# Two-layer transformer block on one core: stick-breaking weights as sums with value steps, outputs copied per head, positions as a column

## The chip, the cores and the metric

The kernel runs on one core of one Trainium2 chip. The metric is the device time of one execution in microseconds (us), the smaller the better. Five engines work side by side on their own instruction streams: TensorE (PE, matmuls, with its weight loads listed apart as PEld), VectorE (DVE), ScalarE (ACT), GpSimd (POOL) and SyncE (SP, which here only issues transfers). They meet through semaphores. Sixteen DMA engines move data between HBM and the on-chip memory, and within the latter.

## What is computed

A sequence of 512 tokens, 1024 wide, passes a hybrid layer (a state-space branch and a stick-breaking attention branch, gated and merged) and a second layer (sparse attention, a gated linear recurrence, a feed-forward net). The change is about two places. The first is the attention of the first layer, with 16 heads of 64:

```
log_fail = jnp.where(mask, jax.nn.log_sigmoid(-logits), 0.0)
between = lax.cumsum(log_fail, axis=3, reverse=True) - log_fail
w = jnp.where(mask, jnp.exp(jax.nn.log_sigmoid(logits) + between), 0.0)
outs.append(jnp.einsum('bhqk,bkhd->bqhd', w.astype(v.dtype), v[:, :kend]))
```

So the weight of key k is sigmoid(logit k) times the product of (1 - sigmoid) over the later keys. The second place is the compression of keys and values in the second layer, where a learned position is added to every block of 32 tokens before a matmul:

```
blocks = blocks + pos[None, None, :, None, :]
flat = blocks.transpose(0, 1, 3, 2, 4).reshape(B, ncmp, G, CMP_LEN * dh)
return jax.nn.gelu(flat @ w1) @ w2
```

## The kernel before

All fp32 weights are streamed in blocks of 1 MB (two pieces of 512 KB, `wraw`). ACT rounds a piece to `whi` (L1152), DVE takes the rest into `wlo` (L1481), and PE does three matmuls for each product (high by high, high by low, low by high), all at L739, which is the helper `mm`. `plan` writes down one list of steps; each engine runs through the same list and does its own part of every step. `weave` spreads two or more lists evenly through each other. So every engine has its order fixed in the program, and the engines wait only on semaphores.

The step ("sb", u) is one unit of the stick-breaking attention: u = 4 h + qt is head h and the query tile qt of 128 rows, with 128 (qt + 1) keys. The 64 units are woven with the slices of eight blocks of products `gate_ssd`, one slice (6 matmuls of 512 columns) a unit. In step u:

- PE: the logits of unit u in bank 4 or 5; the transposes of unit u - 2 (L1087) in bank 6; the products of unit u - 3 with the values, in a quarter of bank 7, which wait for the copy of the unit ahead (`s_o`).
- ACT: two sigmoids of unit u (L1287, L1288), a part of the next head's rounded keys and queries (`stack`, L1271 to L1275), the copy of the turned weights of unit u - 2 (L1297).
- DVE: the rests for the next head (L1902, L1905), a scan of unit u (L1925) that makes the products of "fail" from the last key down, and the copy of the output of unit u - 3 (L1932, 64 x 128).
- POOL: the product of the scan's result with the sigmoid (L2047). PE's transposes wait for it (`s_wgt`).

The values `vt` are read out of PSUM by ACT (L1226), four tiles for each half of the 16 heads: those of half 0 end in the middle of the steps that normalize y, those of half 1 just before unit 0. Results of the `gate_ssd` blocks are read by ACT (L1170) and DVE (L1537, kind `y_ssd`), into `mg`. The arena is one piece of memory of 96 KB a partition, in which tensors lie over each other in turn: `mg` starts at 16 KB, `sb_sig`, `sb_fail` and `sb_w` lie at 48, 52 and 57 KB.

In the second layer the step ("positions",) stands between the slices of the block `kv`. There PE multiplies 32 columns of positions with the compression weights `w1`, one row of output each; ACT copies the row (L1389), and `compress` (0) adds it to the blocks' products by a matmul of one row (`posr`, `one`). Around it, the tiles of the normed input `mix` are turned (PE, L800) and split (ACT L1262, DVE L1674), tile by tile.

Of the kernel before, what the change touches and what calls it, by code (L numbers as in the profile page):

```python
# [23 lines left out]
ALU = mybir.AluOpType  # L24
ACT = mybir.ActivationFunctionType
# [55 lines left out]
def plan():  # L81
# [93 lines left out]
    steps += kv[:2] + [("positions",)] + rows_[7] + kv[2:4] + rows_[8] + kv[4:5] + rows_[9] + kv[5:6] + rows_[10] + kv[6:]  # L175
# [77 lines left out]
def plan_tiles():  # L253
# [27 lines left out]
    groups = {"turn": (4, 6, 7), "dt": (7,), "level": (2, 3), "hout": (2, 3), "turn_qk": (2, 3), "hq": (0, 1), "hf": (0, 1)}  # L281
# [113 lines left out]
BANK_LOGITS, BANK_WT, BANK_O = 4, 6, 7  # L395

# [21 lines left out]
def emit(nc, dram, spill, out):  # L418
    ctx = ExitStack()
    with ctx:  # L420
# [85 lines left out]
        junks = {"x": mem(0, [NT, D]), "y": mem(52, [NT, D])}  # L506
# [9 lines left out]
        sb_fail = mem(52, [2 * 516])  # L516
        sb_w = mem(57, [3, T])
        sb_wT = mem(63, [2, T])
        zeros = mem(67.5, [1])
# [13 lines left out]
        kc2 = mem(24, [2, 2, T])  # L533
# [14 lines left out]
        posr = mem(55, [2 * P])  # L548
# [58 lines left out]
        s_qk, s_sig, s_scan, s_wgt = sem("s_logits"), sem("s_sb_sigmoids"), sem("s_sb_products"), sem("s_sb_weights")  # L607
# [129 lines left out]
        def _(pe):  # L737
# [97 lines left out]
            def positions():  # L835

                pe.wait_ge(s_late, 80)
                for b in range(2):
                    for j in range(CL // 2):
                        last = mm(bank[5][0:1, P * b:P * b + P], pos[:, b, j:j + 1], w1[b][:, j, :], j == 0, j == CL // 2 - 1)  # L840
                last.then_inc(s_pos, 1)

            def compress(i):

                if i == 0:
                    pe.wait_ge(s_kc2, 64)
                    pe.wait_ge(s_posr, 1)
# [45 lines left out]
            def nsa(u):  # L893
# [17 lines left out]
                def summed(v, b):  # L911
                    qt, h = divmod(v, NH)
                    out_ = bank[BANK_O]
                    if h == 0 and b == 0:
                        if qt == 0:
                            pe.wait_ge(s_cpt, NT)
                            pe.wait_ge(s_zero, 2)
# [146 lines left out]
            def stick(u):  # L1064
# [17 lines left out]
                if 0 <= v < SH * NT:  # L1082
                    pe.wait_ge(s_wgt, v + 1)
# [6 lines left out]
                if 0 <= v < SH * NT:  # L1090
# [3 lines left out]
                    if v >= 1:  # L1094
                        pe.wait_ge(s_o, v)
# [1031 lines left out]
```

## Time and profile before

| | |
|---|---|
| median of 3 runs | 1477.96 us (1476.66 to 1478.06) |
| profiled execution | 1475.07 us, of which the span from the first to the last instruction is 1473.2 us |
| PE busy | 1396.8 us (95%), 6981 matmuls |
| DVE busy | 770.7 us (52%) |
| ACT busy | 583.7 us (40%) |
| POOL busy | 178.2 us (12%) |
| mean granted clock of PE | 0.987 of full speed |
| DMA | 119.68 MB, 81 GB/s over the span |

The time follows PE: it is busy for most of the span, and the chain of work that ended last is 82% PE. A change of its order or a wait taken off another engine counts as far as PE stops waiting for it. The busy time of a matmul is longer than the distance to the next one, since they overlap.

### The profile page before, as it was taken

The numbers are of one execution on the slowest core, as the hardware profiler recorded it, in microseconds if no ns is written. First come the engines' busy times: TensorE is split into PE (matmuls) and PEld (weight loads), VectorE is DVE, ScalarE is ACT, GpSimd is POOL, SyncE is SP. The second block draws the span as 40 slices with busy tenths as digits, with TensorE's granted clock in tenths as the row PEclk, the third lists the DMA queues.
The fourth block names the chain that finished last, engine by engine and source line by source line (L and its number), as shares of the span: only waits on it lengthen the run. The fifth ranks groups of instructions, "written<-read, shape, count | busy, mean of one in ns | idle before, by whom it ended". The sixth has DMA issues, their size and how long they took to land.

```text
span 1473.2 us, 17942 instructions
## 1 busy us (share of the span) xinstructions
PE 1396.8 (95%) x6981; PEld 1137.7 (77%) x6981; DVE 770.7 (52%) x1198; ACT 583.7 (40%) x1061; POOL 178.2 (12%) x147
## 2 busy tenths in 40 slices
PE   6899999999999999998999989899989999999999
PEld 4778778877777788876787767677867888888887
DVE  5775454447776564345444657547743433443443
ACT  4544333456666433235325444343333221322221
POOL 0108430003333200000000122121000000000000
PEclk9999999999999999999999999999999999999999
DMA  4222212221111244322331100000522323233222
GB/s 155 84 74 63 81 60 98 86 86 58 44 44 57 70 175 137 107 83 68 139 113 58 44 15 29 15 15 1 172 71 73 100 91 108 88 100 101 93 93 101
DMA packets 34403, 119.68 MB, mean 81 GB/s; under 512 B 3856, under 2 KB 5136, under 8 KB 34064
## 3 DMA queue, kind: packets, MB, share of 16 engines
q1 hardware_dynamic: 33744, 117.50, 24.0%
q10 hardware_dynamic: 576, 1.05, 0.3%
q8 instruction: 56, 0.92, 0.2%
q14 instruction: 27, 0.22, 0.0%
HBM read 113.29 MB, written 4.19 MB: 80 GB/s over the span
## 4 chain that ended last, share of the span: by engine, by line
PE 82%; DVE 10%; ACT 4%; issue 3%; DMA 0%; POOL 0%; DVEq 0%; SPq 0%; ACTq 0%
PE bank L739 79%; DVE wlo L1481 1%; PE bank L800 1%; DVE arena L1925 1%; PE bank L908 1%; PE bank L1087 1%; DVE arena L1500 1%; ACT arena L1258 1%; DVE arena L1649 1%; DVE arena L1932 0%; DVE arena L1773 0%; ACT a_hi L1262 0%; DVE arena L1804 0%; ACT L1239 0%; ACT L1170 0%
## 5 line engine op out<-in xcount | busy, mean ns | idle before, releaser
L739 PE MATMUL bank<-a_hi,whi 128*128 128x512 f32 x848 | 341.8, 403 | 0.7 <-DVE a_lo L1674 0.7
L739 PE MATMUL bank<-a_hi,wlo 128*128 128x512 f32 x848 | 332.4, 392 | 0.0
L739 PE MATMUL bank<-a_lo,whi 128*128 128x512 f32 x848 | 331.7, 391 | 0.0
L1481 DVE TENSOR_TENSOR wlo<-wraw,whi 128x1024 fp32r<-128x1024 f32 x194 | 248.6, 1293 | 54.4 <-ACT whi L1152 48.9
L1152 ACT ACTIVATE whi<-wraw 128x1024 fp32r<-128x1024 f32 x194 | 197.1, 1045 | 184.3 <-PE bank L739 176.8
L739 PE MATMUL bank<-arena 128*128 128x128 f32 (+7 forms) x1400 | 221.4, 304 | 26.7 <-DVE arena L1932 10.1
L739 PEld LDWEIGHTS bank<-arena 128*128 128x128 f32 (+2 forms) x1400 | 175.8, 190 | 58.0 <-issue 29.5
L739 PEld LDWEIGHTS bank<-a_hi,wlo 128*128 128x128 f32 x848 | 160.0, 189 | 34.5
L739 PEld LDWEIGHTS bank<-a_hi,whi 128*128 128x128 f32 x848 | 160.6, 189 | 33.1 <-issue 2.0
L739 PEld LDWEIGHTS bank<-a_lo,whi 128*128 128x128 f32 x848 | 160.6, 189 | 31.7 <-issue 1.0
L739 PE MATMUL bank<-whi,a_hi 128*128 128x512 f32 x320 | 127.3, 398 | 5.2 <-DVE a_lo L1985 3.0
L739 PE MATMUL bank<-whi,a_lo 128*128 128x512 f32 x320 | 124.9, 390 | 0.0
L739 PE MATMUL bank<-wlo,a_hi 128*128 128x512 f32 x320 | 124.9, 390 | 0.0
L2047 POOL TENSOR_TENSOR arena<-arena 128x128 f32<-128x128 f32 (+1 forms) x64 | 67.1, 1053 | 229.6 <-DVE arena L1925 229.6
L739 PE MATMUL bank<-whi,b_hi 128*128 128x512 f32 x240 | 94.8, 395 | 0.0
L739 PE MATMUL bank<-whi,b_lo 128*128 128x512 f32 x240 | 94.1, 392 | 0.0
L739 PE MATMUL bank<-wlo,b_hi 128*128 128x512 f32 x240 | 94.1, 392 | 0.0
L1925 DVE TENSOR_TENSOR_SCAN arena<-arena 128x128 f32<-128x128 f32 (+1 forms) x64 | 54.2, 847 | 50.5 <-ACT arena L1288 50.3
L739 PEld LDWEIGHTS bank<-whi,a_hi 128*128 128x128 f32 x320 | 60.4, 189 | 18.1 <-issue 6.2
L1201 ACT ACTIVATE b_hi<-arena 128x512 fp32r<-128x512 f32 x30 | 19.0, 632 | 135.6 <-DVE arena L1584 123.7
L2040 POOL TENSOR_TENSOR arena<-arena,stat 128x256 f32<-128x256 f32 (+3 forms) x32 | 40.1, 1253 | 254.4 <-DVE stat L1734 254.4
L1574 DVE TENSOR_TENSOR arena<-arena,bank 128x512 f32<-128x512 f32 x32 | 22.0, 687 | 92.4 <-PE bank L739 92.4
(236 smaller groups left out, 1769.0 us busy)
## 6 DMA issues: line engine op xcount, KB each, us to landing
wraw<-in_wblk SPq DMA_DIRECT2D x190, 512.0 KB, 3.7
arena<-in_x SPq DMA_DIRECT2D x4, 512.0 KB, 5.6
arena<-in_x SPq DMA_DIRECT2D x1, 2048.0 KB, 8.3
spill<-arena SPq DMA_DIRECT2D x4, 512.0 KB, 6.7
arena<-spill SPq DMA_DIRECT2D x1, 2048.0 KB, 9.8
out<-arena SPq DMA_DIRECT2D x8, 256.0 KB, 2.5
arena<-in_w1k SPq DMA_DIRECT2D x1, 1024.0 KB, 7.2
arena<-in_w1v SPq DMA_DIRECT2D x1, 1024.0 KB, 6.0
```

The source lines that it names most:

```text
L739: return nc.tensor.matmul(o, lhsT, rhs, start=start, stop=stop, **kw)
L800: last = nc.tensor.transpose(bank[BANK[g]][:, P * i:P * i + P], src[:, t, c0 + P * i:c0 + P * i + P], ident)
L908: last = nc.tensor.transpose(bank[BANK_WT][:, o:o + P], np_[v % 3][:, b_, P * kb:P * kb + P], ident)
L1087: last = nc.tensor.transpose(bank[BANK_WT][:, P * kb:P * kb + P], sb_w[:, v % 3, P * kb:P * kb + P], ident)
L1152: A(whi[n % 2][:, cols], wraw[i][:, 0:cols.stop - cols.start], ACT.Copy).then_inc(s_hi, 1)
L1201: A(b_hi[:, c, :], tt[:, p % 2, :], ACT.Copy).then_inc(s_tround, 1)
L1258: A(junk[:, t, :], src[:, t, :], ACT.Square, accum_out=nss[name][:, t:t + 1]).then_inc(s_ss, 1)
L1481: v.tensor_tensor(wlo[n % 2][:, cols], wraw[i][:, 0:cols.stop - cols.start], f32(whi[n % 2][:, cols]), ALU.subtract).then_inc(s_lo, 1)
L1574: v.tensor_tensor(x, x, ps[:, :], ALU.add).then_inc(s_end["V"], 1)
L1925: v.tensor_tensor_scan(w[:, ::-1], fail[:, ::-1], zeros.to_broadcast([P, kend]), 1.0, ALU.mult, ALU.add)\
L2040: g_.tensor_tensor(w, w, f2[:, 2 * (u % 2):2 * (u % 2) + 2].unsqueeze(2).to_broadcast(list(w.shape)), ALU.mult)\
L2047: g_.tensor_tensor(w, w, sb_sig[:, u % 2, 0:kend], ALU.mult).then_inc(s_wgt, 1)
```

## The change

In the attention, the weights are no longer formed. The sum over keys of weight times value is written by parts: the scan now runs state = fail x state + sigmoid, from 0, which gives for each key the sum of the weights of this and all later keys, and the values are replaced by their steps from one token to the next, v(k) - v(k - 1). The product by POOL goes, and PE's transposes wait for the scan (`s_scan`).

The steps need the value of the token before, which lies on the partition before. So ACT, when it has read the last tile of a half, issues two transfers from on-chip memory to on-chip memory into `v_before[half]`: 127 partitions x 4 x 512, shifted by a partition, and the 3 rows that cross from one tile to the next. POOL zeroes the first row ahead, and subtracts behind (128 x 2048 a half, `s_dv`). `v_before[0]` lies at 52 KB, over `sb_fail` and `sb_w`; `v_before[1]` lies at 16 KB, under `mg`. So ACT's first sigmoid waits for `s_dv` 1, and DVE's first read of a `y_ssd` tile waits for `s_dv` 2.

The outputs of a head stay in one bank, 7 for even and 3 for odd heads, and DVE copies them once a head (64 x 512). The `gate_ssd` tiles use banks 0 to 2 only. The first `z_sb` block waits for the last head's copy.

The positions become a 65th column of the compression's input (`kc2`), so the step ("positions",) and the matmuls of one row go; ACT copies two columns out of PSUM and adds them as the bias of the Gelu. Other sizes, loops and blocks stay.

```diff
-    steps += kv[:2] + [("positions",)] + rows_[7] + kv[2:4] + rows_[8] + kv[4:5] + rows_[9] + kv[5:6] + rows_[10] + kv[6:]
+    steps += kv[:2] + rows_[7] + kv[2:4] + rows_[8] + kv[4:5] + rows_[9] + kv[5:6] + rows_[10] + kv[6:]
...
-    groups = {"turn": (4, 6, 7), "dt": (7,), "level": (2, 3), "hout": (2, 3), "turn_qk": (2, 3), "hq": (0, 1), "hf": (0, 1)}
+    groups = {"turn": (4, 6, 7), "dt": (7,), "level": (2, 3), "hout": (2, 3), "turn_qk": (2, 3), "hq": (0, 1), "hf": (0, 1),
+              "gate": (0, 1, 2), "y_ssd": (0, 1, 2)}
...
+BANKS_STICK = (7, 3)
...
-        junks = {"x": mem(0, [NT, D]), "y": mem(52, [NT, D])}
+        junks = {"x": mem(0, [NT, D]), "y": mem(60, [2, 512])}
...
+        v_before = [mem(52, [NT, 512]), mem(16, [NT, 512])]
...
+                if TILES[g][0] == "z_sb":
+                    pe.wait_ge(s_o, SH)
...
                     for b in range(2):
-                        o = bank[4][:, 64 * b:64 * b + 64].rearrange("p (a b) -> p a b", b=32)[:, :, 0:NCMP]
                         for j in range(CL // 2):
-                            mm(o, w1[b][:, j, :], kc2[:, b, :, 2 * j:2 * j + CS * (NCMP - 1) + 1:CS], j == 0, False)
-                        last = mm(o, posr[0:1, P * b:P * b + P], one[0:1, 0:2 * NCMP].rearrange("p (a b) -> p a b", b=NCMP),
-                                  False, True)
+                            last = mm(bank[4][:, P * b:P * b + 2 * 32 + 1], w1[b][:, j, :],
+                                      kc2[:, b, 2 * j:2 * j + CS * 2 * 32 + 1:CS], j == 0, j == CL // 2 - 1)
...
-                    pe.wait_ge(s_wgt, v + 1)
+                    pe.wait_ge(s_scan, v + 1)
...
-                    if v >= 1:
-                        pe.wait_ge(s_o, v)
+                    if qt == 0:
+                        pe.wait_ge(s_dv, 1 + h // 8)
+                        if h >= 2:
+                            pe.wait_ge(s_o, h - 1)
                     for kb in range(qt + 1):
-                        last = mm(bank[BANK_O][:, P * (v % 4):P * (v % 4) + P], vt[:, kb, pair],
+                        last = mm(bank[BANKS_STICK[h % 2]][:, P * qt:P * qt + P], vt[:, kb, pair],
                                   sb_wT[:, v % 2, P * kb:P * kb + P], kb == 0, kb == qt)
...
                     A(vt[:, t, 512 * half:512 * half + 512], ps[:, :], ACT.Copy).then_inc(s_end["S"], 1)
+                    if t == NT - 1:
+                        cols = slice(512 * half, 512 * half + 512)
+                        act.wait_ge(*ended(g))
+                        act.wait_ge(s_vz, half + 1)
+                        act.dma_start(v_before[half][1:P, :, :], vt[0:P - 1, :, cols]).then_inc(s_vs[half], 16)
+                        act.dma_start(v_before[half][0:1, 1:NT, :], vt[P - 1:P, 0:NT - 1, cols]).then_inc(s_vs[half], 16)
...
-                        act.wait_ge(s_wgt, u - 1)
+                        act.wait_ge(s_scan, u - 1)
+                    if u == 0:
+                        act.wait_ge(s_dv, 1)
...
+                    A(pos_bias, bank[4][:, 64:64 + P + 1:P], ACT.Copy).then_inc(s_posr, 1)
+                    act.wait_ge(s_posr, 1)
...
                     if kind == "y_ssd":
+                        if i == 0:
+                            dve.wait_ge(s_dv, 2)
                         v.tensor_tensor(mg[:, i, :], ps[:, :], sg, ALU.mult).then_inc(s_end["V"], 1)
...
-                    v.tensor_tensor_scan(w[:, ::-1], fail[:, ::-1], zeros.to_broadcast([P, kend]), 1.0, ALU.mult, ALU.add)\
+                    v.tensor_tensor_scan(w[:, ::-1], fail[:, ::-1], sig[:, ::-1], 0.0, ALU.mult, ALU.add)\
                         .then_inc(s_scan, 1)
...
-                if 0 <= o:
-                    h, qt = divmod(o, NT)
+                if 0 <= o and o % NT == NT - 1:
+                    h = o // NT
...
-                    v.tensor_copy(qf[rows_, h // 2, P * qt:P * qt + P], bank[BANK_O][rows_, P * (o % 4):P * (o % 4) + P]).then_inc(s_o, 1)
+                    v.tensor_copy(qf[rows_, h // 2, :], bank[BANKS_STICK[h % 2]][rows_, :]).then_inc(s_o, 1)
...
-                if s[0] == "sb" and s[1] < SH * NT:
-                    u = s[1]
-                    kend = P * (u % NT + 1)
-                    pool.wait_ge(s_scan, u + 1)
-                    w = sb_w[:, u % 3, 0:kend]
-                    g_.tensor_tensor(w, w, sb_sig[:, u % 2, 0:kend], ALU.mult).then_inc(s_wgt, 1)
+                if s[0] == "stack":
+                    turned = max(SPLITS.index(x) for x in SPLITS if x[:2] == ("turn", "y")) + 1
+                    for half in range(2):
+                        if half == 1:
+                            pool.wait_ge(s_split, turned)
+                        else:
+                            pool.wait_ge(s_y, NT)
+                        g_.memset(v_before[half][0:1, 0, :], 0.0).then_inc(s_vz, 1)
+                    for half in range(2):
+                        steps_ = vt[:, :, 512 * half:512 * half + 512]
+                        pool.wait_ge(s_vs[half], 32)
+                        g_.tensor_tensor(steps_, steps_, v_before[half], ALU.subtract).then_inc(s_dv, 1)
```

What the change does to the order on ACT, at the end of the values and the start of unit 0. Before (L1226 reads a value tile, L1287 and L1288 are the sigmoids of unit 0, the table load in between is ACT's change of function):

```order
L1226 ACTIVATE arena<-bank 128x512 [waits s_tile_summed] x2
L1287 ACT_TABLE_LOAD [waits s_zero]
L1287 ACTIVATE arena<-bank 128x128 [waits s_logits]
L1288 ACTIVATE arena<-bank 128x128
L1271 ACTIVATE rounded_arena<-arena 64x512
```

The same place in the changed kernel (L1228 and L1229 are the two transfers, `s_value_steps` is `s_dv`):

```order
L1223 ACTIVATE arena<-bank 128x512 [waits s_tile_summed] x2
L1228 DMA arena<-arena 127x4x512 [waits s_before_first_zero,s_tile_read_s]
L1229 DMA arena<-arena 1x3x512
L1289 ACT_TABLE_LOAD [waits s_value_steps]
L1289 ACTIVATE arena<-bank 128x128 [waits s_logits]
L1290 ACTIVATE arena<-bank 128x128
L1274 ACTIVATE rounded_arena<-arena 64x512
```

Two transfers have come between, and all that ACT does from unit 0 on stands behind a wait for POOL's first subtraction. The same pair of transfers stands behind the last value tile of half 0, further up.

On DVE, around the first `y_ssd` tile, which comes in unit 7. Before (L1925 is the scan, listed here as SCALAR_TENSOR_TENSOR; L1932 copy of an output, L1905 a rest for the next head, L1537 the `y_ssd` tile):

```order
L1925 SCALAR_TENSOR_TENSOR arena<-arena 128x384 [waits s_sb_turned,s_sb_sigmoids]
L1932 COPY arena<-bank 64x128 [waits s_sb_summed]
L1905 TENSOR_TENSOR rounded_arena<-arena,rounded_arena 64x512 [waits s_stacks_rounded]
L1925 SCALAR_TENSOR_TENSOR arena<-arena 128x512 [waits s_sb_turned,s_sb_sigmoids]
L1932 COPY arena<-bank 64x128 [waits s_sb_summed]
L1537 TENSOR_TENSOR arena<-bank,arena 128x512 [waits s_tile_read_s,s_tile_summed]
```

In the changed kernel (L1924 scan, L1931 copy of a head, L1909 the rest, L1541 the `y_ssd` tile):

```order
L1924 SCALAR_TENSOR_TENSOR arena<-arena 128x384 [waits s_sb_turned,s_sb_sigmoids]
L1931 COPY arena<-bank 64x512 [waits s_sb_summed]
L1909 TENSOR_TENSOR rounded_arena<-arena,rounded_arena 64x512 [waits s_stacks_rounded]
L1924 SCALAR_TENSOR_TENSOR arena<-arena 128x512 [waits s_sb_turned,s_sb_sigmoids]
L1541 TENSOR_TENSOR arena<-bank,arena 128x512 [waits s_value_steps,s_tile_read_s,s_tile_summed]
L1924 SCALAR_TENSOR_TENSOR arena<-arena 128x128 [waits s_sb_turned,s_sb_sigmoids]
```

The copies between scans have gone down to one a head, and the `y_ssd` tile, ahead of the scan of unit 8, now waits for POOL's second subtraction.

## Rows read from the trace of the kernel before

**Rows 1.** Waits of PE between 324 and 510 us: total, times, longest.

```profile
PE bank L739 <- DVE arena L1932: 10.1, 17, 0.8
PE bank L739 <- DVE rounded_arena L1905: 1.7, 8, 0.6
PE bank L1087 <- POOL arena L2047: 0.2, 1, 0.2
```

**Rows 2.** Timeline: start us, duration us, engine, line, operation [idle before, releaser].

```profile
353.51 1.82 DVE L1481 TENSOR_TENSOR wlo<-wraw,whi 128x1024 fp32r<-128x1024 f32 x1
356.19 0.41 PE L739 MATMUL bank<-rounded_arena 128*128 128x128 f32 x2 [0.15 <-DVE rounded_arena L1905]
356.44 0.23 PE L739 MATMUL bank<-cstb 128*128 128x128 bf16 x1
356.51 0.50 PE L1087 MATMUL bank<-cst,arena 128*128 128x128 f32 x3
357.33 0.28 DVE L1932 COPY arena<-bank 64x128 f32<-64x128 f32 x1
357.76 0.68 PE L739 MATMUL bank<-arena 128*128 128x128 f32 x4 [0.76 <-DVE arena L1932]
...
368.85 0.68 PE L739 MATMUL bank<-arena 128*128 128x128 f32 x4 [0.44 <-DVE arena L1932]
```

**Rows 3.** Stretches: length, busy PE, PEld, DVE, ACT, POOL, granted clock, DMA share, GB/s.

```profile
357.00:380.00 23.00, 21.55 (x133) 17.77 (x132) 16.34 (x24) 15.45 (x35) 8.30 (x8) 1.00 0.15 47
1055.00:1108.00 53.00, 45.31 (x200) 36.87 (x198) 24.77 (x36) 16.95 (x27) 0.00 (x0) 0.92 0.25 80
```

**Rows 4.** Groups by line: the scans; busy us, mean ns | idle before.

```profile
L1925 DVE TENSOR_TENSOR_SCAN arena<-arena 128x128 f32<-128x128 f32 (+1 forms) x64 | 54.2, 847 | 50.5 <-ACT arena L1288 50.3
```

**Rows 5.** Timeline: last value tile of half 0, units 0 and 8.

```profile
300.06 0.60 ACT L1226 ACTIVATE arena<-bank 128x512 f32<-128x512 f32 x1 [2.04 <-PE bank L739]
...
325.61 0.28 ACT L1287 ACTIVATE arena<-bank 128x128 f32<-128x128 f32 x1
...
345.84 0.69 DVE L1537 TENSOR_TENSOR arena<-bank,arena 128x512 f32<-128x512 f32 x1
346.44 0.67 DVE L1925 TENSOR_TENSOR_SCAN arena<-arena 128x128 f32<-128x128 f32 x1
...
351.09 0.28 PE L1087 MATMUL bank<-cst,arena 128*128 128x128 f32 x1
```

**Rows 6.** DMA view of 742 to 750 us, where `kcf` goes to `kc2`.

```profile
DMA packets 576, 1.05 MB, mean 131 GB/s; under 512 B 64, under 2 KB 320, under 8 KB 576
...
q10 hardware_dynamic: 576, 1.05, 56.8%
```

**Rows 7.** DMA queue of the page: packets, MB, share of 16 engines.

```profile
q1 hardware_dynamic: 33744, 117.50, 24.0%
```

**Rows 8.** DMA view of 352 to 358 us, 40 slices: GB/s of the weights' load.

```profile
GB/s 0 0 0 0 0 0 0 0 0 0 0 0 0 0 0 0 0 0 0 0 0 0 0 0 0 0 0 0 137 109 82 191 218 246 410 328 382 410 410 246
```

**Rows 9.** Views of single lines: ACT's issues of `kc2`, POOL's 128 x 1024 products; ns min/median/max.

```profile
L1216 ACTq DMA_DIRECT2D arena<-arena x4: 617/704/1352, 742.8 to 744.9; - x4
...
L2022 POOL TENSOR_TENSOR arena<-arena,stat x4: 1899/1904/2352, 109.9 to 185.7; 128x1024 f32<-128x1024 f32 x4
```

**Rows 10.** Timeline around the step of the positions.

```profile
699.79 7.15 PE L739 MATMUL bank<-arena,cst 128*1 128x128 f32 x64
704.32 1.22 DVE L1481 TENSOR_TENSOR wlo<-wraw,whi 128x1024 fp32r<-128x1024 f32 x1
...
711.00 1.29 DVE L1674 TENSOR_TENSOR a_lo<-bank,a_hi 128x512 fp32r<-128x512 f32 x2 [5.47 <-ACT a_hi L1262]
711.84 0.47 PE L739 MATMUL bank<-whi,a_hi 128*128 128x512 f32 x1 [1.07 <-DVE a_lo L1674]
715.26 1.09 PE L800 MATMUL bank<-cst,arena 128*128 128x128 f32 x8 [0.41 <-DVE arena L1649]
```

**Rows 11.** Timeline at the start of the compression.

```profile
771.10 0.43 PE L739 MATMUL bank<-cst,arena 1*128 1x62 f32 x2
```

More of the change, by code:

```diff
@@ L532, in emit @@
         kcf = mem(48, [2, T])
-        kc2 = mem(24, [2, 2, T])
+        kc2 = mem(23.75, [2, 2 * T + CL])
         w1 = [mem(56, [CL // 2, P]), mem(72, [CL // 2, P])]
@@ L547, in emit @@
         nsq = mem(54.25, [P])
-        posr = mem(55, [2 * P])
+        pos_bias = mem(55, [2])
         np_ = [mem(kb, [2, T]) for kb in (24, 28, 60)]
@@ L606, in emit @@
         s_attn, s_yd, s_y, s_st = sem("s_ssd_attn"), sem("s_y_diag"), sem("s_y_read"), sem("s_state")
-        s_qk, s_sig, s_scan, s_wgt = sem("s_logits"), sem("s_sb_sigmoids"), sem("s_sb_products"), sem("s_sb_weights")
+        s_qk, s_sig, s_scan = sem("s_logits"), sem("s_sb_sigmoids"), sem("s_sb_sums")
+        s_vz, s_dv = sem("s_before_first_zero"), sem("s_value_steps")
+        s_vs = [sem(f"s_values_shifted{i}") for i in range(2)]
         s_tr, s_wT, s_pv, s_o = sem("s_sb_turned"), sem("s_sb_wT"), sem("s_sb_summed"), sem("s_sb_out")
@@ L833, in qkturn @@
                 last.then_inc(s_tile, 1)
[L835 to L841, printed above, removed]
             def compress(i):
@@ L1111, in _ @@
                     qkturn(*s[1:])
-                if s[0] == "positions":
-                    positions()
                 if s[0] == "compress":
@@ L1215, in tile @@
                             for later in range(2):
-                                act.dma_start(kc2[HD * later:HD * later + HD, :, g_, 0:T - later],
+                                act.dma_start(kc2[HD * later:HD * later + HD, :, T * g_:T * g_ + T - later],
                                               kcf[HD * g_:HD * g_ + HD, :, later:T]).then_inc(s_kc2, 16)
@@ L1254, in norm @@
                         cols = slice(512 * g, 512 * g + 512)
-                        last = A(junk[:, t, cols], src[:, t, cols], ACT.Square, accum_out=nss[name][:, 2 * t + g:2 * t + g + 1])
+                        last = A(junk[:, g, :], src[:, t, cols], ACT.Square, accum_out=nss[name][:, 2 * t + g:2 * t + g + 1])
                     last.then_inc(s_ss, 1)
@@ L1387, in _ @@
                     round_small("gates")
-                    act.wait_ge(s_pos, 1)
-                    A(posr[0:1, :], bank[5][0:1, 0:2 * P], ACT.Copy).then_inc(s_posr, 1)
                 if s[0] == "qkturn":
@@ L1914, in stick @@
                     if u == 0:
-                        for i in range(2):
-                            v.memset(sb_fail[:, 516 * i + 512:516 * i + 513], 1.0)
-                        v.memset(zeros, 0.0).then_inc(s_zero, 1)
-                        dve.wait_ge(s_zero, 1)
                         v.memset(zerob[:, :], 0.0).then_inc(s_zero, 1)
@@ L1948, in _ @@
                 if s[0] == "pos":
+                    dve.wait_ge(s_late, 80)
+                    v.tensor_copy(kc2[:, :, 2 * T:2 * T + CL:2], pos).then_inc(s_pos, 1)
                     v.tensor_scalar(V("q_norm"), V("q_norm"), SCALE, None, ALU.mult)
```

22 lines of the change are left out of this document (9 added, 13 removed).

## The prediction

> **What bounds the kernel now.** I read the page first: PE is busy for nearly the whole span, so only what PE waits for, or what is put in its way, can change the time. Then the waits of PE in the attention stage, 324 to 510 us [rows 1]: 10.1 us for DVE's copies of the outputs, 1.7 us for the next head's rest, and only 0.2 us for POOL. The product by POOL is thus not on the path, though the change is named for it; the copies are, since the products of a unit may not begin before the last unit's copy, and DVE has a scan ahead of that copy. The timeline shows one such place [rows 2]: the transposes start at 356.51, DVE's copy ends at 357.61, the products start at 357.76, after 0.76 us of idle. The pattern comes back every 22.9 us (two heads), with a second, smaller wait (0.44 us at 368.85) and 0.15 us before the logits at 356.19.
>
> **What the change takes out of the attention.** Without a wait a matmul starts some 0.16 us before the listed end of the one ahead (356.44 + 0.23 against 356.51 [rows 2]), so a wait costs its idle time and 0.16. From unit 8 on (346 us) there are 7 waits of 0.76, 6 of 0.44 and 7 of 0.15: 7 x 0.92 + 6 x 0.60 + 7 x 0.31 = 12.2 us. The first two kinds go, since the products now wait for a copy two heads back. The third goes as well: the rest of the next head was late behind an L1481 of 1.82 us [rows 2], and without POOL's work beside it I expect that near the 1.22 of [rows 10]. DVE is busy for 16.3 us of such a stretch of 23 and ACT for 15.5 [rows 3], so neither becomes the bound; the scan with two real operands I take as long as before, a mean of 847 ns [rows 4] (bounds: no change, and twice that, a rival below). The first two heads give 0.9 + 0.6 more, if nothing else holds them. At the end of the stage the last head's copy (as the 0.69 us of L1537 [rows 5]) must end before `z_sb` begins, while POOL's product leaves that path: I set this to nothing, between 0.5 of gain and 0.7 of loss.
>
> **What the change adds: the shifted values.** This is the term that decides. The last tile of half 0 is read at 300.06 to 300.66 [rows 5]. Then 127 x 4 x 512 floats, 1.04 MB, go from on-chip memory to on-chip memory. ACT's first sigmoid, now at 325.61, waits for that and for POOL; DVE's first `y_ssd` tile, now at 345.84 [rows 5], waits for the second half. The question is how long such a transfer takes. The nearest one is that of `kc2`: 576 packets, 64 of them under 512 B, for 4 transfers of 128 rows [rows 6]. So each sends 128 rows and 16 small packets, one for each of the 16 engines that share it, 8 rows each. All transfers of this kernel have 128 or 64 partitions, which 16 divides. Of 127 rows no equal share is possible but one engine with all of them, or 127 with one. No row shows what happens then, so I bound it. Shared by 16 engines as `kc2` was, the 1.04 MB take the 8 us of that window at most. On one engine they take what the engines together were busy for: 0.568 x 16 x 8 = 73 us by `kc2`'s rate [rows 6]; 0.240 x 16 x 1473.2 / 117.5 x 1.04 = 50 us by that of the weights [rows 7]; 41 us at the best slices of a load, 410 GB/s by 16 engines, 25.6 each [rows 8]. I take one engine, and 50 us: the lone transfer has no fifteen neighbours to share the memory's ports with, as `kc2` had, but meets the weights' own packets on its engine.
>
> The Trainium skill has a rule for this, in "DMA: Bandwidth & Descriptors", section "Why a DMA increments its semaphore by 16 and not by 1": a transfer from ACT's or SP's queue is spread over the largest number of engines up to 16 that divides the slowest dimension of both sides, and 127 partitions get a single engine. What this case's trace has, 16 small packets each for transfers of 128 rows, agrees, and no run here yet shows 127. By the bandwidth per engine in that page's table (some 27 GiB/s) the 1.04 MB would take about 36 us, an estimate, and the sum below would come to about 1488; the rates in the rows are lower.
>
> The two halves use the same queue and engine, so the second waits for the first: they land at 300.7 + 50 = 350.7 and 400.7. POOL's subtraction of 128 x 2048 costs two of the 1.90 us in [rows 9], 3.8. The first sigmoid comes near 355 (29 us late), the first `y_ssd` tile at 404.5 where it stood at 345.84: 58.7 us late, and this second wait holds the first within it. What is queued behind: DVE's scan of unit 8 and all later scans; PE's transposes of unit 8 wait for it. PE has some room: the scan ended at 347.1, the transposes began at 351.09 [rows 5], so 4.0 us are taken up. PE comes out 54.7 us late. Having stood still it starts at a lower clock: the stretch from 1055 to 1108, with waits in it, was granted 0.92 on the mean [rows 3], 4 us lost in 53; for the one restart that counts I take 2 us (0 to 4). ACT's issues cost 0.7 us each at the median, 1.35 at most [rows 9]; in this case the wait covers them.
>
> The shared queue of weights feels the second stream on one engine only, 8 of its packets a piece; its loads have slack in a stage that stands still.
>
> **What the change takes out of the second layer.** The step of the positions holds PE for 7.1 us from 699.79 on [rows 10]. What follows doesn't simply move up, since DVE's split of the next tile queues behind its L1481, which ends at 705.54, where it now begins at 711.00 [rows 10]. So the split begins 5.5 us earlier, and the rest of that chain (matmuls 711.84, turn 715.26) hangs on it: 5.5 us gained, of 7.1 at most, 4 at least if DVE has more ahead. The two pairs of one-row matmuls cost 0.35 us each (771.10 to 771.45 [rows 11]); ACT's copy of two columns and its wait give back some 0.3, and the 65th column next to nothing: 0.4 gained. The rest of the second layer is PE without waits, or unchanged.
>
> **Sum.** +54.7 + 2 - 12.2 - 5.5 - 0.4 = +38.6. Against the profiled execution of 1475.07 that is 1513.7; the median of the runs lies 2.9 above that execution, so 1516.5, say 1516.
>
> **The rivals.**
>
> *The transfers are shared by many engines* (the other side of the bound). Then the first half lands by 309 and is subtracted by 313, ahead of 325.61; the second, issued at 324.3, is subtracted by 337, ahead of 345.84. What stays: -12.2 - 1.5 for the first heads - 5.5 - 0.4, and 0.7 of ACT's two issues at the start: -18.9, 1459. It decides as soon as a transfer takes under some 17 us (324.3 + 0.7 + 17 + 3.8 = 345.8). For it: nothing in the trace says that 127 is refused an uneven share. Against: all transfers shown go in equal parts. Chance 0.15.
>
> *Slow packets.* One engine, but at `kc2`'s rate of 73 us: `y_ssd` at 300.7 + 146 + 3.8 = 450.5, so 46 us more, 1562. For it: `kc2` is the only transfer of this kind shown, with the same rows of 2 KB. Against: its sixteen engines ran against each other. Chance 0.12.
>
> *ACT is held by its issue.* 508 rows for one engine may keep ACT at the issue until most are taken; the fourth issue of `kc2` took twice as long as the others [rows 9]. Then ACT stands for nearly 50 us at 300.7 and again at 324: 100 less about 8 of room, less the 20 of the gains: +72, 1550. Against: the rows of one transfer have never held it for more than 1.35 us. Chance 0.13.
>
> *Fast packets*, 41 us: 2 x 9 less, 1498. This is within the likeliest case, as its lower end.
>
> *The scan with two operands is slower*, so that DVE bounds the stage: twice as long, the scans add 54.2 / 8 = 6.8 us for two heads [rows 4] to the 16.3 in 23 and take back the 12 us: 1528. Chance 0.03, within the range.
>
> **How the numbers follow.** One engine, ACT free, 41 to 60 us a transfer: 0.55, 1516, by itself 1497 to 1536. With the rivals above on the slow side (0.28) the range goes to 1568. Below 1495 lies only the shared transfer (0.15) and a little (0.02) between, such as an uneven split over few engines. A measurement of this kernel tells about 0.2% (3 us) from no change. Faster 0.16, same 0.01, slower 0.83.
>
> **What would show it.** Right: landing times of some 50 us for the two transfers; POOL's subtractions near 351 and 401; the first sigmoid behind the first, the `y_ssd` tile behind the second, PE idle for two long stretches; from there on 21.1 us for two heads instead of 22.9, with no wait for the copies; 5.5 us less between the slices of `kv`. Wrong: landings of 5 to 8 us, and no wait for `s_dv` on ACT or DVE. Then the time is near 1459. If ACT has issues of tens of us, it is the third rival.

## The result, and the profile after

The changed kernel takes 1530.45 us (median of 4 runs, 1529.01 to 1531.42) against 1477.31 us (1476.54 to 1478.06) for the kernel before on the same chip: 53.1 us more, ratio 1.036 with a 95% interval of 1.0343 to 1.0376. The profiled execution took 1531.42 us, of which the span is 1529.6.

The page of the profile after: busy time of PE, and the chain that ended last, by line.

```profile
PE 1392.8 (91%) x6909; PEld 1138.3 (74%) x6913; DVE 757.2 (49%) x1148; ACT 582.1 (38%) x1061; POOL 121.7 (8%) x87
...
PE bank L743 76%; ACTq L1229 4%; PE bank L1084 1%; PE bank L806 1%; PE bank L905 1%; DVE arena L1502 1%; DVE wlo L1483 1%; ACT arena L1261 1%; ACT whi L1149 0%; DMA arena<-in_x 0%; DVE arena L1653 0%; DVE arena L1777 0%; DVE arena L1808 0%; ACT a_hi L1265 0%; ACT L1167 0%
```

PE does 4 us less work than before and is idle for the rest. New in the chain is one line with 4%: L1229, an *issue* of a DMA, by ACT. That is the transfer of three rows. The timeline of ACT after, at the place of [rows 5] (L1223 reads a value tile, L1228 issues the 127 rows, L1229 the 3 rows, L1289 is the first sigmoid):

```profile
301.30 0.60 ACT L1223 ACTIVATE arena<-bank 128x512 f32<-128x512 f32 x1 [2.04 <-PE bank L743]
301.93 1.32 ACTq L1228 DMA_DIRECT2D arena<-arena  x1
303.28 34.09 ACTq L1229 DMA_DIRECT2D arena<-arena  x1
337.42 0.60 ACT L1265 ACTIVATE b_hi<-bank 128x512 fp32r<-128x512 f32 x1 [35.52 <-issue]
...
359.91 0.60 ACT L1223 ACTIVATE arena<-bank 128x512 f32<-128x512 f32 x1 [2.12 <-PE bank L743]
360.54 0.74 ACTq L1228 DMA_DIRECT2D arena<-arena  x1
361.32 34.71 ACTq L1229 DMA_DIRECT2D arena<-arena  x1
396.11 1.28 ACT L1289 ACT_TABLE_LOAD   x1 [35.60 <-issue]
397.40 0.28 ACT L1289 ACTIVATE arena<-bank 128x128 f32<-128x128 f32 x1
```

The big transfer is issued in 1.32 us. The next issue on the same queue holds ACT for 34.1 us, and in the second half for 34.7. Read against [rows 5], the delay can be followed: the last value tile of half 0 is read 1.2 us later than before, the last tile of half 1, which stood at 323.69, comes 36.2 later, and the first sigmoid (325.61 before) 71.8 later. PE waits twice, at the turn of the next y tile (L806) and for the first sigmoids (L1290), which must free a bank of logits. Waits of PE after, 296 to 520 us:

```profile
PE bank L743 <- ACT arena L1290: 33.5, 1, 33.5
PE bank L806 <- DVE arena L1650: 33.4, 1, 33.4
PE bank L743 <- ACT arena L1223: 0.9, 1, 0.9
PE bank L1084 <- DVE arena L1924: 0.4, 1, 0.4
```

The 17 waits for copies and the 8 for a head's rest [rows 1] are gone. The stretches after, in the columns of [rows 3]: the two holds, what followed the second, and two heads in full swing:

```profile
303.00:338.00 35.00, 7.37 (x35) 5.83 (x33) 0.00 (x0) 0.58 (x2) 0.00 (x0) 0.64 0.07 25
361.00:396.00 35.00, 3.42 (x18) 2.53 (x17) 0.00 (x0) 0.00 (x0) 0.00 (x0) 0.59 0.08 30
396.00:419.00 23.00, 20.67 (x117) 17.07 (x118) 17.72 (x18) 18.27 (x39) 5.10 (x1) 0.88 0.18 56
430.00:453.00 23.00, 23.00 (x145) 19.31 (x144) 13.70 (x18) 16.12 (x36) 0.00 (x0) 1.00 0.21 65
```

The DMA view of 303 to 338 us shows what moves while ACT is held (the first row is GB/s in 40 slices, q10 is ACT's queue):

```profile
GB/s 12 37 14 26 26 26 26 26 26 23 26 23 26 26 23 26 26 23 26 23 26 26 23 26 23 26 26 23 26 26 23 26 26 23 26 23 26 26 23 26
...
q10 hardware_dynamic: 414, 0.85, 6.4%
```

A flat 25 GB/s, and a share of 6.4% of sixteen engines, which is 1/16 and no more: one engine works and fifteen stand still. POOL, which waits for both transfers of a half, shows when they have landed:

```profile
349.50 4.61 POOL L2054 TENSOR_TENSOR arena<-arena 128x2048 f32<-128x2048 f32 x1
405.08 5.10 POOL L2054 TENSOR_TENSOR arena<-arena 128x2048 f32<-128x2048 f32 x1 [50.98 <-DMA arena<-arena]
```

The first of them shows only that the landing was over by 349.5: POOL's memset of 0.52 us, which had waited for DVE, stands right ahead of it. The second waited for the transfer itself, until 405.1. So the landings are at most 47.5 us and 44.5 us behind the starts of their issues.

### The profile page after: what moved, and what is told of

Its sections match the earlier page's. It is cut to its first block, busy times and chain, and to the rows that moved or that the text cites. A ratio compares the mean times of both kernels' runs of the same rounds, so it can differ in the third digit from the quotient of the medians.

```text
span 1529.6 us, 17658 instructions
## 1 busy us (share of the span) xinstructions
PE 1392.8 (91%) x6909; PEld 1138.3 (74%) x6913; DVE 757.2 (49%) x1148; ACT 582.1 (38%) x1061; POOL 121.7 (8%) x87
## 4 chain that ended last, share of the span: by engine, by line
PE 79%; DVE 9%; ACTq 5%; ACT 4%; issue 2%; DMA 0%; SPq 0%; DVEq 0%
PE bank L743 76%; ACTq L1229 4%; PE bank L1084 1%; PE bank L806 1%; PE bank L905 1%; DVE arena L1502 1%; DVE wlo L1483 1%; ACT arena L1261 1%; ACT whi L1149 0%; DMA arena<-in_x 0%; DVE arena L1653 0%; DVE arena L1777 0%; DVE arena L1808 0%; ACT a_hi L1265 0%; ACT L1167 0%
## 5 line engine op out<-in xcount | busy, mean ns | idle before, releaser
L743 PEld LDWEIGHTS bank<-a_hi,whi 128*128 128x128 f32 x848 | 161.0, 190 | 34.1 <-issue 2.0
L1924 DVE TENSOR_TENSOR_SCAN arena<-arena 128x128 f32<-128x128 f32 (+1 forms) x64 | 56.9, 890 | 93.7 <-ACT arena L1290 93.4
L806 PE MATMUL bank<-cst,arena 128*128 128x128 f32 x144 | 26.5, 336 | 60.8 <-DVE arena L1650 33.8
L806 PEld LDWEIGHTS bank<-cst,arena 128*128 128x128 f32 x144 | 21.3, 174 | 67.2 <-DVE arena L1650 34.6
L743 PEld LDWEIGHTS bank<-whi,a_lo 128*128 128x128 f32 x320 | 61.4, 192 | 13.2
```

Of the source, the lines that this page charges most:

```text
L743: return nc.tensor.matmul(o, lhsT, rhs, start=start, stop=stop, **kw)
L806: last = nc.tensor.transpose(bank[BANK[g]][:, P * i:P * i + P], src[:, t, c0 + P * i:c0 + P * i + P], ident)
L1924: v.tensor_tensor_scan(w[:, ::-1], fail[:, ::-1], sig[:, ::-1], 0.0, ALU.mult, ALU.add)\
```

## The experiments

**The parts alone, and the transfer without its size of 127.** Four kernels on one chip; before took 1476.54 us (1475.3 to 1478.05, 15 runs). One row less in the big transfer:

```diff
-act.dma_start(v_before[half][1:P, :, :], vt[0:P - 1, :, cols]).then_inc(s_vs[half], 16)
+act.dma_start(v_before[half][1:127, :, :], vt[0:126, :, cols]).then_inc(s_vs[half], 16)
+act.dma_start(v_before[half][127:128, :, :], vt[126:127, :, cols]).then_inc(s_vs[half], 16)
```

> The changed kernel with one row less in each big transfer: 126 rows in one transfer and the 127th row in one of its own, so three issues a half and not two; all else as it is. Theory A (the number of rows decides: 127 has no divisor up to 16 but 1, 126 is divided by 14): the 126 rows go over 14 engines, each sends 36 rows of 2 KB where one sent 508, so a half lands within 4 to 8 us, no issue holds ACT for more than 1.4 us, and neither the first sigmoid nor the first y_ssd tile waits; with the gains of the rest that is 1459 us (1456 to 1465). Theory B (the shift by a partition, or the way within on-chip memory, makes the transfer slow, whatever its rows): the 126 rows take 45 us as the 127 did, ACT is held behind them, and the time stays near 1530 us. Theory C (the extra transfers and POOL's subtraction matter by themselves): between, 1480 to 1510 us.

Measured: 1465.49 us (1464.99 to 1467.59), ratio 0.9928 (0.9916 to 0.9941). A single row decides between 3.6% slower and 0.7% faster. That is theory A in kind, 0.5 us above its range. In the DMA view of 300 to 310 us the same megabyte goes by within 6 us, and its packets take 34% of sixteen engines' time. In the timeline the second half's three issues take 0.93, 0.64 and 1.61 us (I had set 1.4 as the most):

```profile
q10 hardware_dynamic: 532, 1.05, 34.1%
```

```profile
326.67 0.93 ACTq L1228 DMA_DIRECT2D arena<-arena  x1
327.63 0.64 ACTq L1229 DMA_DIRECT2D arena<-arena  x1
328.30 1.61 ACTq L1230 DMA_DIRECT2D arena<-arena  x1
330.31 1.28 ACT L1290 ACT_TABLE_LOAD   x1 [3.67 <-issue]
```

The order of the two transfers turned round, the 3 rows first:

> The changed kernel with the two transfers of a half in the other order: the 3 rows first, the 127 rows behind them. In the changed kernel the issue of the 127 rows took 1.3 us and the next issue, of the 3 rows, 34 us. Theory A (an issue is held while the queue still has the rows of the one ahead, so the hold belongs to whatever is issued next): ACT is free after half 0's big issue at about 304 us, is held at half 1's small issue from about 324 to 337 us, and issues the big one then; it lands 45 us behind the first half's landing at 347, so near 392, POOL has subtracted by 397.5, and the first y_ssd tile stands there where it stood at 416.1: 18.6 us less than the changed kernel, 1512 us (1508 to 1518), which is the case that the prediction took as the likeliest. Theory B (the hold is the cost of the small transfer itself): ACT is held for 34 us at the first small issue as well, and the time stays near 1530 us. Theory C (ACT stands behind the big transfer whatever comes next, and the hold only shows at the next instruction): the big issue is followed by 34 us of ACT idle, and the time stays near 1530 us.

Measured: 1515.54 us (1514.83 to 1517.14), ratio 1.0267 (1.0253 to 1.0281). That is theory A: ACT goes on at once behind the big transfer, and is held at its next issue, whatever that is. Here that is the small transfer of half 1, 22 us later (timeline of ACT; the first of its lines is half 0's big issue):

```profile
302.89 0.77 ACTq L1229 DMA_DIRECT2D arena<-arena  x1
303.71 0.60 ACT L1265 ACTIVATE b_hi<-bank 128x512 fp32r<-128x512 f32 x1 [2.21 <-PE bank L806]
...
325.45 19.77 ACTq L1228 DMA_DIRECT2D arena<-arena  x1
345.25 0.72 ACTq L1229 DMA_DIRECT2D arena<-arena  x1
358.93 1.28 ACT L1289 ACT_TABLE_LOAD   x1 [33.51 <-POOL arena L2054]
```

The hold ended at 345.2 and not at 337 as I expected: the stream shared its engine with four loads of weights here, where in the changed kernel no load ran during the first hold. POOL's subtractions began at 354.4 and 399.9, and the first `y_ssd` tile waited 25.5 us for the second and stood at 404.5, 11.6 us earlier than in the changed kernel. The 19.8 us of the hold cost nothing of their own. The landing that ACT's sigmoid waits for came later still, and the second transfer was in the queue by 346.0, while some 100 rows of the first were still to go, so it did not start later for the hold.

The positions alone, on the kernel before:

> The kernel before with one part of the change alone: the positions as a 65th column, no step of the positions, Gelu with a bias; attention as before. Theory A (the DVE split of the next tile hangs on the L1481 ahead of it, and moves up by 5.5 us; 0.4 from the one-row matmuls): 5.9 us less than before, ratio 0.9960. Theory B (what the two traces show between the turns around this place, 21.4 us before and 16.8 after): 4.6 us less, with 0.4 for the compression 5.0, ratio 0.9966. Theory C (the weights' stream or DVE's order takes it back later): 0 to 2 us less. Theory D (all 7.1 us of the step are gained): 7.5 us less, ratio 0.9949.

Measured: 1472.89 us (1472.57 to 1474.73), ratio 0.9977 (0.9968 to 0.9986): 3.65 us less, by the interval 2.1 to 4.7. The timeline of PE behind the turn (L800) that follows the removed step:

```profile
703.94 1.04 PE L800 MATMUL bank<-cst,arena 128*128 128x128 f32 x8
707.80 0.47 PE L739 MATMUL bank<-whi,a_hi 128*128 128x512 f32 x1 [2.83 <-DVE a_lo L1663]
...
709.05 0.63 PE L739 MATMUL bank<-whi,a_lo 128*128 128x512 f32 x1
```

The wait for the split grew from 1.07 [rows 10] to 2.83, as the working said. What it did not have is the third line: 1.2 us behind that wait the matmuls begin to take 0.63 us, and start 0.42 apart, where they took 0.39 and started 0.23 apart: the lower of PE's two clock levels, 1.2 GHz (granted 0.92 on the mean of 697 to 718 us; 1.00 in the like stretch before, 696 to 717). From the turn ahead of the place to the first matmul behind the turn that follows it are 16.8 us (697.52 to 714.33) where there were 21.4 (696.00 to 717.41), a gain of 4.6. In the compression the one-row matmuls are gone, but PE then waits 1.02 us for the Gelu where it waited 0.17, because ACT copies the two columns first: 0.1 of gain instead of 0.4. That is theory B for the place. Place and compression together make 4.7, which lies at the edge of the interval. In the median 1 us is missing, and where it went is not shown.

The copies alone:

> The kernel before with one part of the change alone: two banks for the outputs, one copy a head of 64 x 512, gate_ssd tiles on banks 0 to 2; scan from 1, POOL's product with the sigmoid and the positions as before, values as they are. Theory A (the waits for the copies were the whole cost, 10.1 us with 0.16 us of restart for each, and the 0.15 us waits before the logits stay or go): 10 to 14 us less than before, ratio 0.9905 to 0.9932, and the waits of PE for the copies vanish from the stage. Theory B (POOL's product, which stands between scan and transposes, becomes the next bound once the copies are gone): waits of PE for POOL of several us take their place, and 2 to 7 us are gained. If A holds, writing the weights as sums with steps of values buys nothing by itself.

Measured: 1465.52 us (1464.84 to 1466.73), ratio 0.9925 (0.9912 to 0.9939): 11.0 us less. That is theory A. Waits of PE, 324 to 510 us (L1936 is the copy of the last head, L1909 the rest, L2051 POOL's product):

```profile
PE bank L741 <- DVE rounded_arena L1909: 1.7, 8, 0.6
PE bank L1091 <- POOL arena L2051: 1.2, 1, 1.2
PE bank L741 <- ACT arena L1230: 0.9, 1, 0.9
PE bank L741 <- DVE arena L1936: 0.9, 1, 0.9
```

10.1 us of waits for copies became 0.9. The 1.7 for the rests stayed: they do not hang on the copies. In the changed kernel, without POOL's product, they are gone.

**What is left of the split kernels.** The parts add to 1461.9; the kernel with 126 and 1 rows has them all and takes 3.6 more. Four kernels on one chip (before 1477.35, 1476.43 to 1481.17).

> The changed kernel with 14 rows less in each big transfer: 113 rows in one and 14 in a second; all else as it is. 113 is a prime number as 127 is, 126 is not. Theory A (only the divisors of the number of rows decide how many engines a transfer gets): the 113 rows go over one engine again, though 14 rows were taken off where one row was enough with 126; they take 113/127 of the 45 us, 5 us less a half, and the hold at the next issue is 5 us shorter as well: 1530.5 less 10, 1520 us (1515 to 1526). Theory B (127 is a special case, a full tile less one row, or it is a matter of the last row alone): 113 rows are spread as 126 were, and the time is 1465 us.

Measured: 1521.53 us (1520.97 to 1522.02), ratio 1.03 (1.0285 to 1.0316). That is theory A, to 1.5 us: 113 rows go over one engine like 127, and the holds are 29.49 and 30.29 us.

> The changed kernel with each big transfer in 112 and 15 rows, over 16 and 15 engines by the divisors, where the run with 126 and 1 had 14 and 1. Theory A (with many engines the transfer itself is off the path; what is left over the sum of the parts, 1461.9, is the three issues ahead of unit 0 on ACT, 3.6 us of PE's wait for the first scan): the same time as the 126 and 1, 1465.5 us (1463.5 to 1467). Theory B (the single row on one engine and the 14 engines were a part of the rest): 1461 to 1463 us.

Measured: 1467.75 us (1466.19 to 1469.69), ratio 0.9937 (0.9922 to 0.9952). It is no better than 126 and 1, 0.75 us above the range of theory A, and by ratio not told apart from 126 and 1: the lone row was no part of the rest.

> The kernel before with both parts that gained by themselves, the copies a head and the positions as a column, and without the third: scan from 1, POOL's product, values as they are, no shifted values. Theory A (the parts add: 11.0 and 3.65 us less, from 1476.5): 1461.9 us, ratio 0.990, and so 3.6 us better than the changed kernel with its transfers split well, which has every part. Theory B (the sums with steps save something that the two parts alone don't, such as POOL's 0.2 and 1.2 us of wait): equal to the split kernels, 1465 us or more.

Measured: 1462.33 us (1460.87 to 1463.59), ratio 0.9899 (0.9885 to 0.9914). That is theory A: the two parts add.

The issues moved to POOL (the same transfers, in POOL's program, with half 0 subtracted before half 1 is issued):

> The changed kernel with the shifted values in three transfers a half (112, 15 and the 3 rows), all issued by POOL, which stands idle there, instead of ACT, and with POOL's subtraction of half 0 ahead of the transfers of half 1. Theory A (ACT's issues of 3.3 us ahead of the table load and the first sigmoid are what the split kernels still lose): the first sigmoid comes 3.3 us earlier than at 331.6, near 328, PE's wait of 3.6 us for the first scan goes, and the time is 1461 to 1462.5 us. Theory B (POOL's issues take longer than ACT's, 5 us or more a transfer): the second half is then subtracted after 345.8, the first y_ssd tile waits for it, and the time is 1465 to 1480 us.

Measured: 1465.2 us (1464.34 to 1465.76), ratio 0.9917 (0.9901 to 0.9934). By its time it is neither theory A nor, by its cause, theory B. The first sigmoid moved up to 326.36, earlier than A had it, POOL's issues took 0.5 to 1 us, and the time stayed. The timelines of POOL and DVE say why (L2053 subtraction, L1903 a head's rest, L1672 the split of a y tile, read from PSUM):

```profile
310.49 4.63 POOL L2053 TENSOR_TENSOR arena<-arena 128x2048 f32<-128x2048 f32 x1 [6.68 <-DMA arena<-arena]
...
332.56 4.52 POOL L2053 TENSOR_TENSOR arena<-arena 128x2048 f32<-128x2048 f32 x1 [5.22 <-DMA arena<-arena]
```

```profile
310.99 0.69 DVE L1672 TENSOR_TENSOR b_lo<-bank,b_hi 128x512 fp32r<-128x512 f32 x1 [1.92 <-ACT b_hi L1259]
...
332.63 5.00 DVE L1903 TENSOR_TENSOR rounded_arena<-arena,rounded_arena 64x512 fp32r<-64x512 f32 x1
```

The rest of a head, 0.69 us elsewhere, took 5.00, and ended 0.55 behind POOL's subtraction; PE waited 4.2 us for it. The split L1672, with one operand in PSUM, ran beside the other subtraction in its normal 0.69. The Trainium skill states this as a rule ("SBUF — State Buffer", section "SBUF: two separate sides"): DVE and GpSimd share a pair of ports that the first to start holds for its whole instruction, and a DVE operation wants it when both of its inputs are in SBUF. The rows agree on both counts.

**The subtraction in pieces.** The same two kernels with POOL's instruction of 128 x 2048 made of sixteen; before took 1476.31 us (1475.08 to 1477.67).

```diff
-g_.tensor_tensor(steps_, steps_, v_before[half], ALU.subtract).then_inc(s_dv, 1)
+for piece in range(16):
+    a, b = piece // 4, slice(P * (piece % 4), P * (piece % 4) + P)
+    last = g_.tensor_tensor(steps_[:, a, b], steps_[:, a, b], v_before[half][:, a, b], ALU.subtract)
+last.then_inc(s_dv, 1)
```

> The kernel with 126 and 1 rows (1465.5 us), with one change: each of POOL's two subtractions of 128 x 2048 is made of 16 instructions of 128 x 128. In the 126 and 1 kernel the second subtraction ran from 333.66 to 338.19, and DVE's two scans that began at 334.36 show 5.22 us where they should take 1.4; PE waited 3.6 us for them. Theory A (a single long POOL instruction keeps DVE out of the on-chip memory for its whole length, and short ones let it in between): no DVE instruction there is longer than 2 us, the wait of 3.6 us shrinks to below 1, and the time is 1462 to 1463.5 us. Theory B (the 3.6 us come from ACT's three issues ahead of the first sigmoid, 3.3 us): the time stays at 1465 to 1466 us. Theory C (16 instructions with their fixed costs, 16 x 0.46 = 7.4 us, are as long as one, and DVE is slowed for as long): 1465 us or more, with several DVE instructions a little longer.

Measured: 1465.63 us (1462.92 to 1466.74), ratio 0.9925 (0.9911 to 0.9939). The scans beside POOL are down from 5.22 for two to 0.97 and 1.04, and PE's wait from 3.6 to 1.6. But the median is that of theory B, and the five runs lie 3.8 us apart. The trace is of an execution of 1463.47 us, 2.2 below the median, and the one it is compared with was the slowest of its five, at 1467.59. With ACT's issues in place this run settles nothing by its time.

> The kernel in which POOL issues the transfers (112, 15 and 3 rows; 1465.2 us), with each subtraction of POOL in 16 instructions of 128 x 128. There the first sigmoid came at 326.4 as it should, and yet PE waited 4.2 us, for a DVE instruction (the rest for the next head, 64 x 512) that took 5.00 us, from 332.63 on, where others of it take 0.69, beside POOL's subtraction of 332.56 to 337.08. Theory A (DVE is kept out for the length of one POOL instruction): this wait goes, and the time is 1461 us (1459.5 to 1462.5), the best with all parts of the change in it. Theory B (it is the amount of POOL's work that slows DVE): 1464 to 1466 us. If A holds here and not with ACT's issues, both causes are in the rest.

Measured: 1458.54 us (1458.28 to 1459.64), ratio 0.9882 (0.9866 to 0.9897). That is theory A in kind, 1 us below its range. The same DVE instruction beside POOL's pieces:

```profile
332.02 0.84 DVE L1903 TENSOR_TENSOR rounded_arena<-arena,rounded_arena 64x512 fp32r<-64x512 f32 x1
```

PE's waits of 296 to 510 us come to 2.0 us in all. The 6.7 us between the two medians are more than the wait of 4.2: the stretch from 324 to 346 us was granted 0.84 of the full clock with the whole subtraction and 1.00 with the pieces, which is up to 3.5 us more (0.16 x 22, an estimate). So a stop of DVE for some 4 us cost PE its wait and, behind the wait, part of its clock. By the time, both causes are in the rest: pieces alone (with ACT's issues) and POOL's issues alone each left it at 1465, both together took it away. This is the fastest of the kernels run. Against copies and positions alone, 1462.33, which had its own runs of before, the intervals of the two ratios just overlap; if the 3.8 us between the medians are real, they are what the sums with steps buy by themselves, and the rows have 2.9 for them: the waits for the rests (1.7) and for POOL's product (1.2), which copies and positions alone still have, are gone.

> The kernel with POOL's issues and subtractions in pieces, but with the 127 rows in one transfer again, as in the changed kernel; so only the engine that issues it differs, and the size of the subtraction's pieces. Theory A (the transfer of 127 rows goes over one DMA engine whoever issues it): 45 us each, ACT is never held, the first y_ssd tile waits until both have landed and are subtracted, near 395 to 400 (or later, if POOL issues the second only behind the subtraction of the first, at about 354: then 354 + 45 + 7 = 406), and the time is 1515 to 1525 us. Theory B (POOL's queue divides a transfer in another way than ACT's, over all engines): no wait of its own, and the same time as with 112 and 15 rows, near 1461 us.

Measured: 1541.7 us (1540.09 to 1542.51), ratio 1.0441 (1.0426 to 1.0456). That is theory A in kind, 17 us above its range. Timeline of POOL:

```profile
301.25 4.78 POOL L2048 DMA_DIRECT2D arena<-arena  x1 [68.07 <-ACT arena L1223]
306.04 0.55 POOL L2049 DMA_DIRECT2D arena<-arena  x1
359.89 6.62 POOL L2054 TENSOR_TENSOR arena<-arena 128x128 f32<-128x128 f32 x16 [53.31 <-DMA arena<-arena]
...
367.71 4.61 POOL L2048 DMA_DIRECT2D arena<-arena  x1 [0.74 <-POOL arena L2044]
372.32 0.53 POOL L2049 DMA_DIRECT2D arena<-arena  x1
422.86 6.62 POOL L2054 TENSOR_TENSOR arena<-arena 128x128 f32<-128x128 f32 x16 [50.01 <-DMA arena<-arena]
```

Counted from the start of the issue, as for ACT's queue, POOL's transfers take 58.6 and 55.2 us where ACT's took 47.5 and 44.5. The issue of the 127 rows is 4.6 to 4.8 us long, where that of 112 rows costs 0.8 to 1. The DMA view of 305 to 340 us has the rest of the difference (q0 is POOL's queue, q1 that of the weights):

```profile
DMA packets 4569, 2.70 MB, mean 77 GB/s; under 512 B 3917, under 2 KB 3917, under 8 KB 4569
q0 software_dynamic: 3993, 0.60, 20.9%
```

Where 112 and 15 rows made 320 packets a half, 127 rows make some 4100, nearly all of them under 512 B. From 306 to 315 us they take 66% of sixteen engines' time and move 0.12 MB. The load of weights issued meanwhile lands after 12.1 us, where the median is 3.7. The rows themselves go only behind them, over one engine: from 330 to 345 us the queue takes 5.9% of sixteen. What the small packets are for is not shown. And the second transfer starts only at 367.7, so the two waits add: the `y_ssd` tile stands at 429.6, where I had 406.

## Why the prediction held, and which of its steps did not

**One engine for 127 rows** was the step that decided, and it is shown: 6.4% of sixteen engines in the changed kernel, 34% with one row less. 113 rows behave like 127, 126 and 112 like 128. The packets of ACT's queue say it to the engine. A half has 511 rows, and by [rows 6] each transfer adds one small packet for each engine that shares it. The queue sent 515 packets with 127 + 3 rows, 529 with 113 + 14 + 3, 532 with 126 + 1 + 3, and 545 with 112 + 15 + 3. That is 4, 18, 21 and 34 small ones: 1 + 3, 1 + 14 + 3, 14 + 4 + 3 and 16 + 15 + 3 engines. The page cited there, section "Why a DMA increments its semaphore by 16 and not by 1" of "DMA: Bandwidth & Descriptors" in the Trainium skill, gave this rule; the trace agrees for every size run (the lone row goes by its next dimension, of 4). **The rate**, taken as 50 us, was at most 47.5 and 44.5. The best slices of a load [rows 8], 25.6 GB/s an engine, were the right row: a lone transfer runs at 25. The 41 us of that row were its pure time, without the start and the small transfer behind. With loads of weights on the same engine, as in the run with the small transfer first, the first landing came 51.5 us behind its issue, near the 50 of the forecast.

**ACT free** is the step that failed. I took the issue of the 127 rows as done in a microsecond, which it is, and gave 0.13 to ACT being held by it. What happened is that rival, with the hold moved one issue further and shorter: the *next* issue waits until most of the rows are gone. When ACT came free, 406 and 407 of 508 packets had gone in the changed kernel, and 350 and 354 of 452 with 113 rows: each time 98 to 102 were left. So a hold takes 34 us and not 50. The rival's sum, redone with it: two waits of PE, 33.4 + 33.5, less the 14.65 that copies and positions give by themselves, is 52.3; measured 53.1. With ACT free at that place, as in the run with the small transfer first, the time was 1515.5, the 1516 of my forecast, and it came by the forecast's path: landings one behind the other, by 354.4 and 399.9 (350.7 and 400.7 forecast), and the `y_ssd` tile at 404.5. What is luck there are terms that cancel: PE waited 31.4 + 21.5 = 52.9 where 54.7 and 2 for the clock were forecast, and the gains are 14.65 where 18.1 were. The changed kernel itself, at 1530, lies 14 us above the forecast and inside the range, but that is luck of size: two holds happened to cost 14 us more than the wait that the range was made for, and by the sign that the prediction itself names (issues of tens of us) it is the third rival that came.

**The wait of the `y_ssd` tile**, the 58.7 us of my sum, did not occur in the changed kernel: the tile stands at 416.1 with no idle time before it, since the holds had moved everything else further than the landing.

**The attention's gain** of 12.2 is right in size: in full swing two heads take 21.0 us (the transposes of the same unit at 415.56, 436.60 and 457.64) where 21.1 was forecast, and the copies alone gave 11.0. Its third kind of wait, the rests, went with POOL's product as argued, and stayed where only the copies were changed.

**The scan** keeps its duration, a mean of 890 ns against 847 [rows 4], but for the two scans beside POOL's second subtraction. The mean says slower by 5% and the rows say otherwise:

```profile
404.57 5.90 DVE L1924 TENSOR_TENSOR_SCAN arena<-arena 128x512 f32<-128x512 f32 x2 [0.22 <-ACT arena L1290]
```

These two take 1.6 us elsewhere (1.23 and 0.41). The 4.3 on top are more than the 2.7 by which all the scans grew; without those two they are no slower.

**POOL's subtraction**, forecast at 3.8 from the 1.90 of [rows 9], took 4.6 and 5.1, and kept DVE out meanwhile, which no term had: it is a part of what the shared transfers, forecast at 1459, missed by when they came to 1465.5. The other part is ACT's issues, since with these in place the pieces brought nothing. With both removed that rival's 1459 is there, at 1458.5.

**The clock**: a term of 2 us for one restart. The stretches behind the holds were granted 0.81 (338 to 361) and 0.88 (396 to 419), which by the arithmetic of the prediction would be 4.4 and 2.8 us. The sum above leaves 0.8 us for it, so part of the slow stretch may fall into waiting time; this was not separated.

**Positions**: 5.5 forecast, 4.6 at the place. The split's matmuls do come 5.5 us earlier, counted from the turn ahead, and PE's lower clock behind its longer wait takes the rest back. The compression gave 0.1 of 0.4. The two together measured 3.65.

## What to carry to other kernels

Look at the partition count of every transfer, shifted ones above all: shifting a full tile by a partition leaves 127, one engine and 25 GB/s, and taking one row into a transfer of its own gave back 65 us here. Such a transfer costs twice if the engine that issued it has to issue another: put the small one first, and issue from an engine that has nothing else to do. But don't move a transfer of 127 rows to POOL: that was the slowest kernel of all, at 1541.7 us. Count a long POOL instruction with two operands in on-chip memory as time in which DVE may stand still, and cut it into pieces before judging what it costs.

## What the runs showed of the hardware

- ACT is not held by a long issue but by the one behind it, until some 100 packets of 2 KB of the one ahead are left (holds of 34.1, 34.7, 29.5 and 30.3 us).
- A transfer of 127 rows within on-chip memory runs at 25 GB/s on ACT's queue; by POOL's queue it lands 55 to 59 us behind the start of its issue. Of that, the issue takes 4.7 us, and some 3,900 small packets go ahead of the rows, for 9 us on 66% of the sixteen engines.
- One POOL instruction of 4.5 us stretched a DVE instruction from 0.69 to 5.00 us. In the attention before, beside POOL's smaller products, the same is seen on a small scale: the rests of the weights (128 x 1024) between 400 and 500 us took a median of 1.62 us, and 1.20 in the changed kernel, which has no such products.
